# Multiplications of constants ahead of TensorE's waits, in a two-part transformer kernel

## The reference

```python
for l in range(2):                                  # first block
    y = rms_norm(x) @ w_in + b_in                   # 13 slices
    m = mlstm_chunkwise(...)                        # 4 heads of 64
    h = hgrn2_chunkwise(...)                        # 4 heads of 64
    s = swa_sink_attention(...)                     # 8 heads, window 128
    x = x + concat(m, h, s) @ w_out
    x = x + square(relu(rms_norm(x) @ w_up)) @ w_down
    x = x + sigmoid(rms_norm(x) @ w_ple_gate) * rms_norm(p @ w_ple_proj)
for l in range(2):                                  # second block
    h = rms_norm(x) * (1 + scale1) + shift1
    x = x + gate1 * mixer(h)                        # three kinds of attention
    h = rms_norm(x) * (1 + scale2) + shift2
    x = x + gate2 * ((silu(conv(h @ w_g)) * (h @ w_u)) @ w_down)
return rms_norm(x)
```

## Time and profile before

| | |
|---|---|
| runs | 2966.37 us median (2963.68 to 2966.91) |
| profiled execution | 2961.24 us, span 2959.3 us |
| PE busy | 2812.9 us, 95% of the span |
| DVE, ACT, POOL busy | 1612.1, 1122.8, 194.3 us |
| mean granted TensorE clock | 0.963 of full |
| DMA | 278.80 MB, 94 GB/s |

### The profile page before, as it was taken

One profiled execution on the slowest core, in us unless ns is written; L12 is line 12 of the kernel. 1 busy time (PEld: TensorE's weight loads), 2 busy tenths in 40 slices (PEclk: granted clock), 3 DMA queues, 4 the chain that ended last, 5 costly groups with the idle time before them and its releaser, 6 DMA issues. The chain is left out here.

```text
span 2959.3 us, 37023 instructions
## 1 busy us (share of the span) xinstructions
PE 2812.9 (95%) x14756; PEld 2335.6 (79%) x14756; DVE 1612.1 (54%) x2705; ACT 1122.8 (38%) x1708; POOL 194.3 (7%) x192
## 2 busy tenths in 40 slices
PE   6999899999999889999989999899998999899998
PEld 5877788888788667888877878788887887788887
DVE  5755566655765648555575434553534544454443
ACT  6445332323554433322354444332323344332232
POOL 1310100001221110000130000100000000100001
PEclk9987999999999699999999999999998999999999
DMA  4210154343321014444422111223222211122322
GB/s 157 73 44 29 51 185 184 143 171 114 102 79 58 15 60 163 155 163 150 171 89 86 57 34 40 86 82 111 100 78 94 72 42 31 57 100 79 114 82 68
DMA packets 42978, 278.80 MB, mean 94 GB/s; under 512 B 6072, under 2 KB 6456, under 8 KB 11704
## 3 DMA queue, kind: packets, MB, share of 16 engines
q1 hardware_dynamic: 42808, 276.44, 26.8%
HBM read 274.33 MB, written 2.10 MB: 93 GB/s over the span
## 5 line engine op out<-in xcount | busy, mean ns | idle before, releaser
L306 DVE TENSOR_TENSOR low_panels<-raw_panels,high_panels 128x2048 fp32r<-128x2048 f32 (+3 forms) x218 | 471.8, 2164 | 339.1 <-ACT high_panels L293 339.0
L293 ACT ACTIVATE high_panels<-raw_panels 128x2048 fp32r<-128x2048 f32 (+3 forms) x218 | 392.9, 1802 | 465.9 <-PE bank L1551 149.2
L424 PE MATMUL bank<-mlp_h_high,high_panels 128*128 128x512 f32 x1152 | 451.3, 392 | 0.0
L424 PE MATMUL bank<-mlp_h_high,low_panels 128*128 128x512 f32 x1152 | 450.2, 391 | 0.0
L424 PE MATMUL bank<-mlp_h_low,high_panels 128*128 128x512 f32 x1152 | 448.7, 390 | 0.0
L424 PEld LDWEIGHTS bank<-mlp_h_low,high_panels 128*128 128x128 f32 x1152 | 216.4, 188 | 46.0
L424 PEld LDWEIGHTS bank<-mlp_h_high,low_panels 128*128 128x128 f32 x1152 | 216.3, 188 | 45.7
L424 PEld LDWEIGHTS bank<-mlp_h_high,high_panels 128*128 128x128 f32 x1152 | 216.4, 188 | 44.4
L451 PE MATMUL bank<-high_panels,h_high 128*128 128x256 f32 x704 | 206.2, 293 | 0.5 <-ACT values_and_ones L2069 0.5
L424 PE MATMUL bank<-h_high,high_panels 128*128 128x512 f32 x496 | 202.7, 409 | 2.0 <-DVE h_low L1431 1.7
L1551 PE MATMUL bank<-mlp_hid_high,high_panels 128*128 128x512 f32 x512 | 203.2, 397 | 0.0
(11 more groups left out here) (345 smaller groups left out, 5095.6 us busy)
## 6 DMA issues: line engine op xcount, KB each, us to landing
raw_panels<-in_w SPq DMA_DIRECT2D x236, 1024.0 KB, 4.8
raw_panels<-in_w SPq DMA_DIRECT2D x16, 384.0 KB, 3.1
raw_panels<-in_w SPq DMA_DIRECT2D x4, 960.0 KB, 4.7
raw_panels<-in_w SPq DMA_DIRECT2D x4, 768.0 KB, 4.1
row<-in_row SPq DMA_DIRECT2D x2, 1220.0 KB, 6.1
x<-in_xT SPq DMA_DIRECT2D x2, 1024.0 KB, 6.3
raw_panels<-in_w SPq DMA_DIRECT2D x4, 512.0 KB, 3.5
mix<-in_rope SPq DMA_DIRECT2D x2, 1024.0 KB, 6.2
```

What stands on the lines that cost most here:

```text
L293: self.nc.scalar.activation(self.g.high[:, j % SPLIT, 0:raw.shape[1]], raw, ACT.Copy).then_inc(self.high_ready, 1)
L306: self.nc.vector.tensor_tensor(self.g.low[:, j % SPLIT, 0:w], raw, self.g.high[:, j % SPLIT, 0:w].bitcast(F32), ALU.subtract).then_inc(sel ...
L424: ins = nc.tensor.matmul(bank[:, :], w[a][:, k, c0:c0 + P], rhs[b][:, k0 + k, :], start=first and k == 0 and j == 0, stop=last and k == kt ...
```

## The change

A function `keep_running` issues n multiplications of the identity matrix (128x128, float32, the weights) by 256 columns of constants (a block of ones and the identity, which lie side by side in `kc`) into a PSUM bank that nothing is reading. Their result is never used. It is called on TensorE ahead of waits:

- in `sum_partitions`: 5 at the end of the embedding gate, 6 at the end of the second block's MLP; none at the four other ends of a stage;
- in `spread_rstd`: 10 in the very first layer, 4 at the other norms that follow a stage; none in the embedding gate and at the last norm;
- in `project_as_ready`: 5 at all but the embedding gate's;
- in the mLSTM ahead of `block_scores(j)`: 2 at j = 6, 8, 9, 10, 11, 3 at 12, 4 at 13 and 14, 21 in a layer; at j = 6 with one more wait, for DVE to have read the last dense group;
- in the HGRN ahead of `products(k)`: 2, 1 and 6 at k = 15, 16 and 17;
- in the banded attention ahead of `turn_chunk(c)`: 4 at c = 1 and 3 at c = 2, with a wait for the last gate group to have been read.

Nothing is removed or moved.

```diff
+def keep_running(nc, g, bank, n):
+    for _ in range(n):
+        nc.tensor.matmul(bank[:, 0:2 * P], g.ident, g.kc[:, 0:2 * P], start=True, stop=True)
+
-def sum_partitions(nc, pe, g, e):
+def sum_partitions(nc, pe, g, e, running=0):
+    keep_running(nc, g, g.bank[7], running)
     pe.wait_ge(e.sum_used, DC - 1)
...
-def spread_rstd(nc, pe, g, e):
+def spread_rstd(nc, pe, g, e, running=0):
+    keep_running(nc, g, g.bank[7], running)
     pe.wait_ge(e.rstd_ready, 1)
...
-def project_as_ready(nc, pe, w, rhs, banks, full, ready, n=None, before=None):
+def project_as_ready(nc, pe, g, w, rhs, banks, full, ready, n=None, before=None, running=0):
+    keep_running(nc, g, g.bank[7], running)
     for k in range(DC):
...
+                    if j == 6:
+                        pe.wait_ge(kept_v, by_dve[window_groups[-1] + 1])
+                    keep_running(nc, g, bank[2], {6: 2, 8: 2, 9: 2, 10: 2, 11: 2, 12: 3, 13: 4, 14: 4}.get(j, 0))
                     if j >= 2:
                         pe.wait_ge(s("m_probs"), j - 1)
...
+                    if c in (1, 2):
+                        pe.wait_ge(kept_v, by_dve[hg_groups[-1] + 1])
+                        keep_running(nc, g, dense_bank(hg_groups[-1]), 5 - c)
                     if i >= 1:
                         pe.wait_ge(chunk_low, i)
...
-                spread_rstd(nc, pe, g, e)
+                spread_rstd(nc, pe, g, e, running=10 if l == 0 else 4)
...
+                    keep_running(nc, g, bank[0], {15: 2, 16: 1, 17: 6}.get(k, 0))
                     products(k)
...
-                sum_partitions(nc, pe, g, nx)
+                sum_partitions(nc, pe, g, nx, running=5)
...
-                sum_partitions(nc, pe, g, nx)
+                sum_partitions(nc, pe, g, nx, running=6)
```

More of the change, by code:

```diff
@@ L772, in dense @@
                     if i == 0:
-                        project_as_ready(nc, pe, p, (hh, hl), [dense_bank(0), dense_bank(1)], full, e.h_ready)
+                        project_as_ready(nc, pe, g, p, (hh, hl), [dense_bank(0), dense_bank(1)], full, e.h_ready, running=5)
                     if i < 2:
@@ L1532, in _ @@
             def _(pe):
-                spread_rstd(nc, pe, g, e)
+                spread_rstd(nc, pe, g, e, running=4)
                 mods_done = 0
@@ L1539, in _ @@
                     if i == 0:
-                        project_as_ready(nc, pe, w, (hh, hl), [grp.bank(g, 0), grp.bank(g, 1)], full, e.h_ready)
+                        project_as_ready(nc, pe, g, w, (hh, hl), [grp.bank(g, 0), grp.bank(g, 1)], full, e.h_ready, running=5)
                     grp.free(pe, i)
@@ L1683, in _ @@
                         grp.free(pe, DC + 1)
-                        project_as_ready(nc, pe, w, (hh, hl), [grp.bank(g, DC), grp.bank(g, DC + 1)], full, e.h_ready, before={DC - 1: emb_total})
+                        project_as_ready(nc, pe, g, w, (hh, hl), [grp.bank(g, DC), grp.bank(g, DC + 1)], full, e.h_ready, before={DC - 1: emb_total})
                     if c >= 2:
                         project_feature(nc, pe, w, (c % 2) * P, (hh, hl), grp.bank(g, DC + c)).then_inc(full, 1)
-                sum_partitions(nc, pe, g, nx)
+                sum_partitions(nc, pe, g, nx, running=5)
             @block.gpsimd
@@ L2396, in program @@
         kc = sb("kc", [P, K_WIDTH])
+        g.kc = kc
         g.x = sb("x", [P, DC, S])
```

## The result

The changed kernel took 2949.03 us (median of 8 runs, 2937.76 to 2953.29), the kernel before, on the same chip, 2962.28 (8 runs, 2958.67 to 2966.91). The ratio is 0.9941, with a 95% interval of 0.9927 to 0.9955: 17.5 us faster (13 to 22), where 28 were forecast. 2949 lies inside the range, at its slower half, and 1 us above the span given for the forecast case (2928 to 2948). The profiled execution took 2950.95 us.

What follows compares the result with a forecast made beforehand. TensorE, busy in 95% of the span, was taken as the bound, with 219 us at half clock. Terms 16 + 15 + 3.5 - 1.5 - 3.6 - 1.2 = 28 us gave 2933, plus 5.1 for the median: 2938 us, range 2923 to 2956.

Steps and rivals of the forecast that it cites:

- forecast case: Whole kernel: the constants hold the clock and the terms gain 28 us; 2928 to 2948 us, 65%.
- Two of the prediction's own signs: Profile after: calls in the norms should not take 0.85 us; at j = 14 L888 should take 2.45 at 1.00.
- held at the norms, lost in the mLSTM: Rival: clock held at norms but falls behind the mLSTM's four calls at j = 14; 2948 us, 8%.
- Norms, forecast 16: Seven norms between stages: faster spreads and projections at full clock gain 16 us, bounds 25 and 2.
- mLSTM, forecast 15 (bounds 16.5 and 5): mLSTM's second half: results and turns at full clock gain 7.4 and 7.8 us in the two layers, together 15.
- The two calls at j = 6, forecast -0.85 a layer: mLSTM: not covered, since head 0's result stands behind them and DVE waits for it; they cost 0.85 us.
- Attention, forecast 3.5 (9, -2.6): Banded attention: calls at c = 1 and 2 gain 3.5 us, bounds 9 and -2.6.
- HGRN, forecast -1.5: HGRN, steps 16 and 17: the six calls at k = 17 lose 1.5 us for both layers, bounds +1 and -5.
- First norm, forecast -3.6: Very first norm: ten calls take 6.4 us, 4.6 late less 1.0 for a faster spread; bounds -1.5 and -6.
- Last norm, forecast -1.2: Last norm: six calls against a 0.82 us wait, 1.8 late, spread perhaps 1.0 faster; bounds -0.7 and -1.8.
- The rival "with both": Rival: clock hardly held at the norms and also lost in the mLSTM; 2958 us, within the 8% rival.
- Both upper bounds together: Fast end of the 8-in-10 range: norms and mLSTM both at their upper bounds, given as 2924 us.

Runs made afterwards that it cites:

- Experiment 4: Full change with each call's operands cut to 4 partitions, same columns, places and number; 3049.63 us, ratio 1.0283 to the kernel before.
- experiment 1: Full change with only the calls at the seven norms between stages kept, also called seven_norms; ratio 0.9970 to the kernel before, gain 8.9 us.
- experiment 2: Full change with only the mLSTM's calls and the wait at j = 6 kept, also called second_half_only; ratio 0.9966 to the kernel before, gain 10.1 us.
- experiments 3: Full change with only the calls in HGRN and the banded attention kept; ratio 1.0006 to the kernel before, 1.8 us slower.
- 7: Full change without calls at the first norm and its projection, the last norm, HGRN and banded attention; ratio 0.9919 to the kernel before, gain 24.0 us.
- the fastest version: Full change without first-norm, last-norm, HGRN and j = 6 calls; six at j = 14, modulation sums moved later, one call at MLP end; 2935.74 us, ratio 0.9907.

## Why the prediction was right, and where its sizes were off

The mechanism came: the constants hold the clock, at the price per call that was read off two pairs of rows (0.43 at full, 0.85 at half clock), and where it is held the spreads, projections and results take their full-clock times. Experiment 4 shows that it is the clock that pays. Mean clock 0.988 (0.985 or more), projections 11.3 to 11.7 us (11.5) and first spread 34.6 (34) are as forecast. Two of the prediction's own signs came only in part: at two of the seven norms the calls take 0.9 us each, and in the second layer the results (L888 before, L899 now) take 3.00 and 4.37 us instead of 2.45. The gain was 17.5 us instead of 28. That 2949 lies in the range owes as much to the rivals as to the forecast case: it is 1 us from the 2948 of "held at the norms, lost in the mLSTM", whose condition, the clock falling once in each layer, is what the profile after shows, and which had been given 8%. That the number fits so well is partly luck: this rival takes 16 us for the norms and 5 for the mLSTM, and measured are less of the first and more of the second. Term by term:

- **Norms, forecast 16.** In the norms themselves, from reciprocal to last projection, it is 15.4 us over the seven (125.3 before, 109.9 after, worked out from the traces): the term was right there. What failed is the step "what is late next": behind the two norms ahead of an MLP TensorE came up against DVE's modulation sum and gave back 5.4 us in the profiled execution (-1.8 and -1.9 became +1.7 and 0.0), at the first by the wait of 1.67 us and the clock that fell behind it, at the second by a wait of 1.64 us with the clock up. The ledger's seven norms sum to -11.3 (1.3 us of it ahead of the reciprocals), and the runs of experiment 1 give 8.9. In before, DVE ended its modulation at 368.79 and TensorE took the sums at 369.42 without a wait, 0.6 us of slack that the slow projections had made; I had read the idle time ahead of the norm's projections, and not who is waited for behind them.
- **mLSTM, forecast 15 (bounds 16.5 and 5).** A layer in which the clock is held gives 7.1 to 7.3 us with the calls at j = 6, against the one profile of before, so the working (7.4 and 7.8) was right as to what can be had. It is not had every time: the profile after shows 5.7 and 1.2, the runs of experiment 2 show 10.1 for both layers. The mis-sized step is the one taken as certain: that four calls at j = 14 bridge to the end. They leave 1.00 us idle, and then come results whose small products leave TensorE mostly loading weights (12.13 of the 13.42 us above); which of the two lets the clock fall no run separates. The prediction named that as a rival, with 8%; it happened in four of the ten layers with four calls, all of them in change and second_half_only.
- **The two calls at j = 6, forecast -0.85 a layer:** 1.1. They seem to keep the clock from falling over head 0's result (none of ten layers with them, three of eight without), which I had not seen: only their price stood in the sum.
- **Attention, forecast 3.5 (9, -2.6):** 0.6 in the ledger, nothing in experiments 3 and 7. The first stretch of the earlier trace rows now runs at 1.00:

```profile
266.00:280.50 14.50, 11.41 (x74) 8.58 (x73) 9.48 (x34) 9.87 (x25) 0.00 (x0) 1.00 0.00 1
```

  The two stretches don't hold the same work (53 and 74 of TensorE's instructions). For the same work, from the scores at 264.84 (now 266.28) to the dense group at 277.15 (277.54), TensorE's busy time fell from 11.25 to 8.17 us, three calls included, the stretch from 12.31 to 11.26, and DVE's starts behind it moved by only 0.4 us: a pair goes round TensorE, DVE and ACT one after another. The lower bounds by DVE and ACT, which I had seen, should have been the estimate.
- **HGRN, forecast -1.5:** -2.5 (+1.3 and +1.2 in the ledger). The six calls at k = 17 took 2.75 us at full clock in both layers (at 152.96 and 905.03), and all of it is on the path: from the start of step 16 to that of step 17 it takes 3.97 us where the clock is up and no call stands between (seven_norms, second layer), and 6.66 with the clock up and the six calls (second layer after). In before it was 6.88 and 5.58. In the first layer after, the clock fell behind step 16 (149.2 to 152.6) in spite of the calls at k = 15 and 16, and it was 8.18. The operand that the prediction puts at 148.4, 5.2 us behind step 16, can't be what step 17 waits for, since in seven_norms it starts sooner.
- **First norm, forecast -3.6:** -4.4. The ten calls took 7.36 us and not 6.4.
- **Last norm, forecast -1.2:** -1.5. The calls ran at full clock, but the spread got nothing of it (2.08 as before).

  These three lie inside their bounds, all worse than my middle value.

With the measured terms the sum is 11.3 + 10.1 + 0.6 - 2.5 - 4.4 - 1.5 = 13.6 us, against 17.5 (13 to 22) measured. That is inside the interval; where the other 4 us lie is not shown.

Three numbers of the prediction don't follow from its own terms. The rival "with both" is 28 - 14 - 10 = 4, so 2962 and not 2958. Both upper bounds together, 25 and 16.5, give 2966.4 - 38.5 = 2928 and not 2924. And the 0.1% and 0.2% that were taken as the scatter of one kernel's times came from three runs of before; its runs here lie up to 0.9% apart. None of the three moves the result out of or into the range.

## What to carry to other kernels

Constants ahead of a wait pay where TensorE's slow stretch is itself the path and where they fit the wait; read the clock of the stretch behind them and ask which engine sets its pace, since a stretch that goes round several engines gives little back at full clock (0.4 us in the banded attention). Give them out by the wait's length, full-size and enough to leave no idle time before short products, and leave them out where nothing waits behind them: there they cost their full price (HGRN's step 17), and twice that if the clock is down when they start. Then look one wait further: when the slow stretch gets faster, the engine that was just in time behind it is late, and moving the work that waits for it can be worth more than another call (at these two norms moving kept 1.8 us each; the calls lost 0.2 at one and kept 1.3 at the other).

## What the runs showed of the hardware

- The partitions of these products don't change their duration but do bear on the clock: four calls on 4 partitions took 1.96 us as on 128, and the clock stayed at 0.50 through stretches such as the 54.5 us above.
- How much time is spent at half clock differs from execution to execution of one and the same kernel, and the time goes with it. The kernel before ran from 2951.67 to 2979.02 us over all its runs here, about 1%, at mean clocks from 0.966 to 0.957; the fastest version from 2922.24 us at 0.993 to 2948.85 at 0.982. Which stretches they are differs between profiles in code that is the same: the second block's attention, which nothing here touches, took 6.4 us more in one version's profile and 4.9 less in another's than in before's. So a term of 3 us was read from rows and not from medians of six to twelve runs.
- The clock falls not only over idle time: it fell in the middle of a result of 20 products of 65 columns that TensorE went through without a wait inside it (985.4 above, busy 13.42 of 13.70 us while it was down). The last idle time, 1.00 us, had ended 2.3 us earlier, at 983.09.
- Transposes against the identity don't keep it from rising, as the earlier trace rows had shown: in the first layer after, 12 of the 16 instructions of the stretch below are L914's turns (2.75 of its 3.40 us), and behind it the clock went from 0.50 to 1.00:

```profile
234.50:237.90 3.40, 3.40 (x16) 2.85 (x16) 0.59 (x4) 1.20 (x2) 0.00 (x0) 0.50 0.00 0
237.90:243.40 5.50, 4.80 (x60) 4.39 (x58) 0.70 (x3) 2.39 (x4) 0.00 (x0) 1.00 0.01 1
```
